# Feed-forward output projection by seven half-size products, with GpSimd making the combined operands

## The reference

```
h    = rmsnorm(x, norm2_g) * (1 + sc2) + sh2
gate, up = split(h @ w_ffn_in)              # w_ffn_in: 1024 x 5632, so gate and up have 2816 columns each
x    = x + gt2 * ((silu(gate) * up) @ w_ffn_out)     # w_ffn_out: 2816 x 1024
out  = rmsnorm(x, final_g)
```

## Time and profile before

| what | value |
|---|---|
| time, median of 3 runs | 1635.99 us (1635.97 to 1636.31) |
| profiled execution, first to last instruction (span) | 1634.9 us |
| TensorE busy | 1604.4 us, 98% |
| VectorE / ScalarE / GpSimd busy | 909.5 / 640.9 / 260.3 us |
| DMA, mean over the span | 136 GB/s, 223.05 MB |
| TensorE's granted clock, mean | 0.997 |
| feed-forward output, TensorE (chain) | from 1376.90 us on, 1056 matmuls of line 1656 |

### The profile page before, as it was taken

How to read it: one execution, slowest core, us unless ns; L and a number is a source line. 1 busy time by engine, 2 the same in 40 slices (tenths; PEclk the granted TensorE clock), 3 DMA queues, 4 the chain that set the end, 5 groups by cost and what they waited for, 6 DMA issues and landing times.

```text
span 1634.9 us, 23987 instructions
## 1 busy us (share of the span) xinstructions
PE 1604.4 (98%) x8239; PEld 1313.7 (80%) x8239; DVE 909.5 (56%) x1440; ACT 640.9 (39%) x1313; POOL 260.3 (16%) x282
## 2 busy tenths in 40 slices
PE   6999999999999999999999999999999999999998
PEld 5687878888877777878788888788888888888886
DVE  4576655435545454546652489766666666334424
ACT  4334456555544444444212244333333333232413
POOL 1036561011101010100000003223322220000000
PEclk9999999999999999999999999999999999999999
DMA  8826666655733333523545322322222224543412
GB/s 282 276 91 215 202 199 186 201 182 153 227 99 110 98 109 98 161 88 111 168 142 193 109 59 65 111 82 77 77 77 87 92 71 146 213 176 130 148 45 103
DMA packets 223678, 223.05 MB, mean 136 GB/s; under 512 B 19066, under 2 KB 189187, under 8 KB 223619
## 3 DMA queue, kind: packets, MB, share of 16 engines
q1 hardware_dynamic: 216642, 197.12, 37.7%
q0 software_dynamic: 6976, 25.17, 4.0%
HBM read 163.53 MB, written 60.31 MB: 137 GB/s over the span
## 4 chain that ended last, share of the span: by engine, by line
PE 87%; DVE 4%; DMA 3%; POOL 3%; SPq 1%; issue 1%; ACT 1%; DVEq 0%; POOLq 0%; ACTq 0%
PE pm L1642 22%; PE pm L1656 15%; PE ps L1211 13%; PE pd L1501 11%; PE pm L1211 8%; PE pm L1596 3%; PE sc L1454 2%; PE tT L1477 2%; PE tT L1466 2%; PE pm L1554 1%; POOL pr L1124 1%; POOL Xi L1126 1%; PE gps L1391 1%; DMA adab<-in_w_ada_dram 1%; DVE est L2311 1%
## 5 line engine op out<-in xcount | busy, mean ns | idle before, releaser
L1211 PE MATMUL ps<-act_hi,w_hi 128*128 128x512 f32 x448 | 150.0, 416 | 2.6 <-DVE est L2316 1.7
L2225 DVE TENSOR_TENSOR w_lo<-w_raw,w_hi 128x1024 fp32r<-128x1024 f32 x60 | 77.4, 1290 | 123.0 <-ACT w_hi L1751 113.2
L1211 PE MATMUL ps<-act_lo,w_hi 128*128 128x512 f32 x448 | 138.9, 391 | 0.0
L1211 PE MATMUL ps<-act_hi,w_lo 128*128 128x512 f32 x448 | 138.5, 390 | 0.0
L1656 PE MATMUL pm<-act_hi,w_hi 128*128 128x512 f32 x352 | 137.2, 390 | 0.0
L1656 PE MATMUL pm<-act_hi,w_lo 128*128 128x512 f32 x352 | 137.0, 389 | 0.0
L1656 PE MATMUL pm<-act_lo,w_hi 128*128 128x512 f32 x352 | 136.9, 389 | 0.0
L1642 PE MATMUL pm<-act_hi,w_hi 128*128 128x512 f32 x320 | 124.5, 389 | 0.0
L1642 PE MATMUL pm<-act_lo,w_hi 128*128 128x512 f32 x320 | 124.5, 389 | 0.0
L1642 PE MATMUL pm<-act_hi,w_lo 128*128 128x512 f32 x320 | 124.5, 389 | 0.0
L1501 PE MATMUL pd<-act_hi,w_hi 128*128 128x512 f32 x256 | 111.3, 435 | 0.0
(11 more groups left out here) (375 smaller groups left out, 3462.0 us busy)
## 6 DMA issues: line engine op xcount, KB each, us to landing
w_raw<-in_w_in_dram SPq DMA_DIRECT2D x44, 512.0 KB, 5.3
w_raw<-in_w_ffn_in_dram SPq DMA_DIRECT2D x44, 512.0 KB, 3.7
h_raw<-h_d SPq DMA_DIRECT2D x36, 512.0 KB, 3.4
a_raw<-in_w_ada_dram SPq DMA_DIRECT2D x32, 512.0 KB, 4.2
w_raw<-in_w_ffn_out_dram SPq DMA_DIRECT2D x44, 256.0 KB, 3.8
h_d<-hid SPq DMA_DIRECT2D x21, 512.0 KB, 2.7
pk_d<-pk SPq DMA_DIRECT2D x8, 768.0 KB, 3.7
qkva_d<-est POOLq DMA_DIRECT2D x12, 512.0 KB, 6.0
```

The source lines that it names most:

```text
L1211: ins = pe.matmul(dst[:, cols], wt[:, ds % 2, k, :], at[:, cols], start=(first and n == 0), stop=(last and n == 2))
L2225: dve.tensor_tensor(w_lo[:, ds % 2], w_raw[:, ds % NR], w_hi[:, ds % 2].bitcast(F32), ALU.subtract)\
```

## The change

The feed-forward output is computed with seven products too. The operands are taken in pairs of hidden blocks (11 pairs, `NPAIR`), even and odd output blocks, and the two token halves: a 2x2 by 2x2 block product. The seven products stand outermost (in the order P1, P2, P6, P7, P4, P5, P3), the 11 pairs inside, so there are 77 steps. A step multiplies one weight combination of 128x512 (four output blocks) with one hidden combination of 128x512: 4 x 3 = 12 matmuls of 128x512, into four half-banks; the products take the two halves of PSUM in turn. VectorE adds the seven results into the residual `xF` as each product ends.

Three of the seven weight operands are slices of `w_ffn_out`; the other four are sums that GpSimd makes in the loop `D_B` (`mix_out`: four additions of 128x512 a pair, from a 1 MB load and into a 1 MB store to `sm_d`). That loop is therefore written out four times on GpSimd. Three of the seven hidden operands are halves of stored blocks; the other four GpSimd makes in the feed-forward input loop (`mix_hidden`, again four additions of 128x512 a pair, stored to `tq_d`). VectorE's write of a hidden block now also waits until GpSimd has read the one before in that buffer. Raw hidden pieces of 128x512 have six buffers (`hq`). All output rows go through the four buffers of `row_a`, so rows 4 to 7 wait for the stores of rows 0 to 3.

```diff
-        STEPS = 2 * NF
+        NPAIR = NF // 2
+        (X_P1, X_P2, X_P6, X_P7, X_P4, X_P5, X_P3) = range(7)
+        STEPS = 7 * NPAIR
...
+        def pieces_at(t):
+            if t < 7:
+                return {O_P3: (0,), O_P7: (1,), O_P4: (2, 3)}.get(t, ())
+            return range(2 * t - 10, 2 * t - 8) if t < 12 else range(t + 2, min(t + 3, STEPS))
...
@@ SyncE @@
+                k, c = divmod(t, NPAIR)
+                if k in (X_P1, X_P2, X_P4):
+                    j, odd = 2 * c + (k != X_P1), int(k == X_P4)
+                    src = w_ffn_out[j * P:(j + 1) * P, :].rearrange("p (u two q) -> p two u q", two=2, q=P)[:, odd]
+                else:
+                    src = sm_d[c, {X_P5: 0, X_P6: 1, X_P7: 2, X_P3: 3}[k]].rearrange("p (u q) -> p u q", q=P)
+                sp.dma_start(w_raw[:, d, 0:4], src).then_inc(raw_in[d], 16)
...
             for t in range(7, STEPS):
                 load_o(t)
-                if t < NF + 6 or NF + 9 <= t < STEPS - 2:
-                    load_h(t - (3 if t < NF + 6 else 6))
+                for m in range(loaded, min(pieces_by(t - 3) + 6, STEPS)):
+                    load_h(m)
+                    loaded = m + 1
...
+                if 9 <= t < 13:
+                    load_x2(2 * (t - 9))
+                if 14 <= t < 18:
+                    load_x2(2 * (t - 14) + 1)
@@ GpSimd @@
+            def mix_out(c):
+                a = sm_raw[:, :, :].rearrange("p k (u two q) -> p k two u q", two=2, q=P)
+                a11, a21, a12, a22 = (a[:, k, e] for k in range(2) for e in range(2))
...
+                pool.tensor_tensor(m1, a21, a22, ALU.add).then_inc(sm_ready, 1)
+                pool.tensor_tensor(m3, a11, a21, ALU.subtract).then_inc(sm_ready, 1)
+                pool.tensor_tensor(m2, m1, a11, ALU.subtract).then_inc(sm_ready, 1)
+                pool.tensor_tensor(m4, a12, m2, ALU.subtract).then_inc(sm_ready, 1)
+                pool.dma_start(sm_d[c].rearrange("m p q -> p m q"), sm[:, :, :]).then_inc(sm_stored, 16)
+                if c + 1 < NPAIR:
+                    load_mix(c + 1)
+            MIX_AT = {4: 0, 11: 1, 18: 2, 25: 3}
...
+                    if s in MIX_AT and 4 * i + MIX_AT[s] < NPAIR:
+                        mix_out(4 * i + MIX_AT[s])
...
+            with pool.Fori(1, 9) as i:
+                mix_weights(3, i, wait_apart)
+                mix_pair(i)
+                mix_weights(4, i, wait_apart)
@@ TensorE @@
-            def out_part(t, b, h):
+            def out_part(t, u):
...
+                for x, (wt, at) in enumerate(((whi, bhi), (whi, blo), (wlo, bhi))):
+                    ins = pe.matmul(out_bank(k, u), wt[:, u, :], at, start=(c == 0 and x == 0),
+                                    stop=(c == NPAIR - 1 and x == 2))
...
                 if part == 0:
-                    pe.wait_ge(sqs_ready, 10 + 3 * h + 3)
+                    pe.wait_ge(sqs_ready, 7 + 6 * h + 6)
@@ VectorE, after the last step @@
+            for n in range(1, 4):
+                last_add(1, n)
+            sum_p3(0)
+            sum_p3(1)
+            last_add(1, 4)
+            sum_p3(2)
+            last_add(1, 5)
+            sum_p3(3)
+            last_add(1, 6)
+            last_rsqrt(1)
```

More of the change, by code:

```diff
@@ L534, in raw_o, with out_bank, piece, piece_free @@
             return unit(NF, 0) + t
-        def block_of(t):
-            return t if t < NF else STEPS - 1 - t
-        H_SPLITS = [t for t in range(STEPS) if not NF <= t < NF + 8]
-        def out_bank(b, h):
-            return pm[2 * h + b // 2][:, half(b % 2)]
+        def out_bank(k, u):
+            return pm[2 * (k % 2) + u // 2][:, half(u % 2)]
+        def piece(x):
+            s = x % 16
+            cols = half(s // 8)
+            return act_hi[:, s % 8, cols], act_lo[:, s % 8, cols]
+        def piece_free(x):
+            if x < 16:
+                return dense_mm, op_count(NF - 1, (O_P1, O_P2, O_P6, O_P3)[x // 4])
+            return dense_mm, step_count(x - 16)
+        def piece_in(x):
+            return hq_in[x % 6], (64 if x % 6 < 4 else 32) + 16 * (x // 6 + 1)
+        def pieces_at(t):
+            if t < 7:
+                return {O_P3: (0,), O_P7: (1,), O_P4: (2, 3)}.get(t, ())
+            return range(2 * t - 10, 2 * t - 8) if t < 12 else range(t + 2, min(t + 3, STEPS))
+        def pieces_by(t):
+            return sum(len(pieces_at(a)) for a in range(t + 1))
+        def product_end(k):
+            return step_count(NPAIR * k + NPAIR - 1)
+        OUT_SUMS = {X_P1: 1, X_P2: 1, X_P6: 2, X_P7: 3, X_P4: 1, X_P5: 2, X_P3: 1}
+        def out_sum(k, u, j=0):
+            before = 6 * NF + 4 * sum(OUT_SUMS[a] for a in range(k))
+            return before + (2 * u + j if k == X_P5 else 4 * j + u) + 1
+        READY_AT = {0: (0, 2, 4, 6, 1, 3, 5, 7), 1: (1, 3, 5, 7, 0, 2, 4, 6)}
+        def turn_bank(t):
+            return pm[2 + t % 2] if 2 <= t < 6 else pm[t % 2]
         def ada_parts(n):
@@ L1649, in _ @@
                         product(n, o, i)
[L1651 removed]
+            def out_part(t, u):
                 whi, wlo = op_slot(t % 7)
[L1654 to L1657 removed]
+                bhi, blo = piece(t)
+                k, c = divmod(t, NPAIR)
+                for x, (wt, at) in enumerate(((whi, bhi), (whi, blo), (wlo, bhi))):
+                    ins = pe.matmul(out_bank(k, u), wt[:, u, :], at, start=(c == 0 and x == 0),
+                                    stop=(c == NPAIR - 1 and x == 2))
                 return ins
@@ new lines, in _ @@
+                if 33 <= t < 37:
+                    last_square(0, t - 33)
+                    last_scale(0, t - 33)
+                if t == 62:
+                    for n in range(4, KT):
+                        last_square(0, n)
+                    for n in range(4, KT):
+                        last_scale(0, n)
+                if t == 68:
+                    last_row(0)
+                    last_row(1)
+            for n in range(4):
+                last_square(1, n)
+                last_scale(1, n)
@@ L2214, in _ @@
+            last_row(2)
+            last_row(3)
+            for n in range(4, KT):
+                last_square(1, n)
+                last_scale(1, n)
+            for t in range(4, NT):
                 last_row(t, half(1))
@@ new lines, in sum_p5, with sum_p3, last_add @@
+            def sum_p5(u):
+                dve.wait_ge(dense_mm, product_end(X_P5))
+                dve.wait_ge(sum_ready, out_sum(X_P7, u, 2))
+                for b in (2 * u, 2 * u + 1):
+                    add_scaled(b, 1, out_bank(X_P5, u))
+            def sum_p3(u):
+                dve.wait_ge(half_mm, 19 + u + 1)
+                dve.wait_ge(sum_ready, out_sum(X_P5, u))
+                add_scaled(2 * u, 1, out_bank(X_P3, u))
+            def last_add(h, n):
+                dve.wait_ge(sq_ready, 10 + 8 * h + n + 1)
+                if n > 1:
+                    dve.wait_ge(sqs_ready, 7 + 6 * h + n - 1)
+                dve.tensor_tensor(tmp[:, half(h)], tmp[:, half(h)], est[:, n % 2, half(h)], ALU.add)\
@@ L2880, in _ @@
[L2880 to L2895 removed]
+                dve.wait_ge(ft_mm, FT0 + t + 1)
```

424 lines of the change are left out of this document (240 added, 184 removed).

## The result

The changed kernel takes 1614.19 us (median of four runs, 1612.43 to 1616.07) and the one before, run with it, 1635.98 us (1634.22 to 1636.31): a ratio of 0.9867, 95% interval 0.9856 to 0.9879. It is 21.8 us faster. The forecast was 1611.1 us with a range of 1606 to 1620; the time lies inside that, and inside the likeliest case's own range. The profiled run took 1615.57 us with a span of 1613.9. In a second set of four runs the same kernel took 1613.38 us (0.9864, 0.9847 to 0.9880), with a profiled span of 1611.8.

A forecast was written before the change was run, and what follows sets the result against it. TensorE, busy 98% of the span, was taken as the bound. From the profiled 1634.9 us: - 29.9 (matmuls) + 1.0 (start) + 0 + 2.4 (D_B) + 1.6 (tail) = 1610.0, plus 1.1 for the median: 1611.1 us, range 1606 to 1620.

The forecast's parts named there:

- the likeliest case: Whole kernel: the forecast of 1611 us itself, own range 1608.5 to 1615 us, chance 0.56.
- Matmuls removed: Feed-forward output: 924 matmuls in place of 1056, 132 fewer at 0.2267 us each, 29.9 us less.
- The pace of a step: Output stage: VectorE (70%), ScalarE (63%), PSUM halves and steady loads keep up with 2.72 us steps; 0 us of waiting.
- The start burst: Output stage's start: queued loads make step 18's weights barely late; 1 us of TensorE waiting, bounds 0 and 8.
- Additions in the feed-forward input: Feed-forward input loop: GpSimd's four additions a pair fit its idle time, and weight splits are six steps ahead; 0 us.
- Additions in D_B: Loop D_B: GpSimd's additions hold VectorE's `negm` and `Pm` behind `Xm`, 0.8 us in each of three iterations; 2.4 us.
- The tail: After the last matmul: TensorE's last sums wait for an addition and square behind the last residual; 1.6 us more.
- Everything is hidden: Rival, D_B and stage start: GpSimd's pairs miss sensitive VectorE instructions and bandwidth suffices; 1606.8 to 1607.7 us; chance 0.17.
- Pace and lock in full: Rivals: output stage runs at its loads' pace throughout, or GpSimd's holds on VectorE all reach TensorE; over 1632 us, together 0.06.

The follow-up runs named there:

- e5: Changed kernel with the last square addition earlier in the tail, odd residual blocks loaded at steps 30 to 36, GpSimd's D_B pairs at slots 11, 18, 25; 1606.73 us.
- e4: Changed kernel with GpSimd's addition pairs in D_B three an iteration, at slots 4 (right behind `Ct`), 18 and 25, slot 11 left out; 1620.72 us.
- e10: e8 with the first of slot 11's four GpSimd additions in D_B moved up behind `Ct`; 1604.89 us.
- e11: e8 with the first two of slot 11's four GpSimd additions in D_B moved up behind `Ct`; 1601.76 us.
- e8: e5 with the even residual blocks loaded at steps 14 to 17 in place of 9 to 12; 1603.08 us.

## Why the prediction was right, and where not

*Matmuls removed, 29.9 us: right.* With the start cured, the stage takes 214.9 us at 0.2267 us a matmul, 29.7 us less than the 244.6 before.

*The pace of a step: right.* No wait of TensorE between step 16 and the tail, no wait for a half of PSUM. Over the stage VectorE is busy 63% and ScalarE 49%, where the sum said 70 and 63.

*The start burst, 1.0 us: too small; 3.3 us measured (218.0 less 214.7), inside the bounds of 0 and 8.* The place is right (`w_lo` between steps 9 and 22, on full queues), the mechanism only half. I made the sum for step 18 and passed the earlier ones with "more room"; the wait came at step 11. For step 12, due at 32.7 us, I had 8 to 9 MB, and 9 MB at 340 GB/s are ready at 32.8, which is no room at all. In e5 the windows up to the end of the wait, 32.5 us after step 0 began, add up to 9.6 MB for step 11: the loads run ahead of the steps, and what is behind in the program shares the engines with what is due. Each load is then under way for 8 to 14 us. That left the splits of step 11 without lead. The second half is the term that I put at nothing: I had seen that GpSimd's additions can hold VectorE's splits, and passed them with "six steps ahead", for the feed-forward input. At the start of the output stage the lead was gone, and the additions of pair 0 added 1.8 us of a wait of 1.9 in after. About 0.5 us more was lost at the second wait, behind the loads alone, and 0.5 to the lower clock.

*Additions in the feed-forward input, 0: right.* At equal clock the stage takes 350.1 us with them and 350.06 without.

*Additions in D_B, 2.4 us: right in size, 2.0, and wrong in place.* I said that a GpSimd addition costs up to 1.07 us, since `negm` had once ended with `Ct`. The hold need not end with the instruction: `negm` waited for `Ct` and three additions, 4.51 us. I counted each addition as a separate hold and looked only where TensorE's slack was smallest; the row behind `Ct`, which I had passed as having slack enough, used that slack up. That the sum came out is chance: by the same rules e4 should cost no more in D_B than after, and its four iterations take 7.3 us more than before, after's 1.9. I had named three iterations of 82 to 83 us and one of 81.5; two and two came.

The Trainium skill (SBUF — State Buffer, "Who interferes with whom") says of the shared pair that the first to issue has it for the whole instruction and the other blocks fully. The runs agree on who is held: the reduction just before `negm` keeps its 0.69 us. They go beyond it on how long: a waiting instruction can be passed over by several GpSimd instructions in a row, 1.24 us each, as e10, e11 and after show behind `Ct`, and need not be, as slot 11 shows.

*The tail, 1.6 us: right, 1.7 measured, plus 1.2 us of clock in some executions.* That term was in no step.

*What is left.* Of the 3.1 us between forecast and median, 2.3 are the start and 0.1 the tail's order; D_B gives 0.4 back; the rest, about 1, is of the size of the two clock terms (1.2 each), which the runs have or lack. The runs of after spread over 3.6 us; which of them had which was seen only where there is a profile.

*The rivals.* "Everything is hidden" (1606.8 to 1607.7) was false of the change, but it is nearly what e5 measures (1606.7) once tail, odd blocks and slot 4 are moved. Pace and lock in full did not happen.

The best version, e8, takes 1603.08 us: 31.6 less than the 1634.67 of the kernel before in the same call, more than the 29.9 of the matmuls. The rest is mostly the clock, which in e8's profile did not fall at the start of the feed-forward input (348.50 us in place of 350.06, 1.6 us). The pause there, 3.9 us in the earlier trace rows, is 2.9 in every profile of the changed kernels, but this is mostly TensorE arriving later at it, since VectorE's last 13.9 us of work in front of its end are the same in both: the stretch from the first matmul of that line to the end of the pause is 36.2 us in after and e8 and 36.7 before, so only 0.4 us of the 1.0 reach the time.

## What to carry to other kernels

When work is given to GpSimd beside a busy VectorE, take as the worst case not one of its instructions but the row without a gap, and set the whole row against the slack of whatever small VectorE instruction can fall into it; split the row, or put it where VectorE's next such instruction is far. When a stage is shortened, add up the bytes due before each early step, and move those that are needed late; 2.1 MB were enough here, and a second 2.1 MB brought nothing. And look at both together: work ahead hides a hold only as long as the loads let it stay ahead. A pause of TensorE of 1.4 to 3 us can cost 1 to 3 us more behind it through the clock, so a removed pause is worth more than its length.

## What the runs showed of the hardware

- A two-column VectorE instruction (0.17 us alone) took 0.79, 2.04, 3.27 and 4.51 us beside `Ct` with 0, 1, 2 and 3 GpSimd additions following without a gap. Once in e10, and in every pair of four at slot 11, it got in between two instructions of such a row (0.88 us at 546.62 in after).
- VectorE's splits of 128x512, 0.69 us alone, took 1.75 to 1.78 us beside a row of GpSimd additions (e5, e8), and the additions 1.72 to 1.74 in place of 1.27: there the two engines took turns.
- The DMA engines moved 399 to 411 GB/s in stretches of 5 us at a share of 1.05 (e5), where the highest of the earlier trace rows was 354 at 1.08: a full share is not one rate. Over the 27 us from 1380 to the end of the wait the mean is 355, near the 340 that I had taken.
- The same 1536 matmuls took 348.5, 350.1 or 351.3 us, with a granted clock of 1.00, 0.83 or 0.69 to 0.70 in their first 10 us, behind a pause of 2.9 us (3.9 in the kernel before, with 350.1).
